# Attention values of one mixer stage: values as the stationary operand in two column groups, one product for each pair of units, and new orders of the unit loop on three engines

## The chip, the cores and the metric

One core of one Trainium2 chip runs the whole program in one launch. The metric is the device time of an execution in microseconds (us), and the number to be predicted is the median of the changed kernel's executions.

## What is computed

The reference is a network of two blocks on 256 tokens of width 1024. The first block has two layers, and each layer runs a feed-forward, a hybrid mixer, an attention over 256 memory tokens and a second feed-forward. The second block has two layers of sparse attention and a feed-forward with squared ReLU. The change lies in the hybrid mixer, which runs twice (once in each layer). What matters of it:

```
s_s = einsum('bqgrd,bqgmd->bqgrm', qi, ks) * scale - slopes * dist    # selected keys (all keys here)
o_s = einsum('bqgrm,bqgmd->bqgrd', masked_softmax(s_s), vs)
s_w = einsum('bqgrd,bkgd->bqgrk', qi, kw) * scale - slopes * dist     # window keys (all keys here)
o_w = einsum('bqgrk,bkgd->bqgrd', masked_softmax(s_w), vw)
o   = gs0 * o_c + gs1 * o_s + gs2 * o_w                              # gates; o_c: compressed keys
```

There are 8 heads of width 64 in 2 groups of 4 heads, and each group shares one set of keys and values. With 256 tokens both branches see every earlier token. The mixer's output goes through a root-mean-square norm, is joined with the output of a retention branch and multiplied by `w_out`. The keys and values of the memory attention (`xa_wk`, `xa_wv`) don't depend on the mixer, and the kernel computes them between the mixer's small steps.

## The kernel before

Large products are in three parts: each weight item of 128 x 2048 numbers is loaded by SyncE (SP) into one of four raw buffers, ScalarE (ACT) writes its rounded high part (`whi`), VectorE (DVE) writes the rest (`wlo`), and TensorE (PE) multiplies high by high, high by low and low by high. The items are taken in a fixed order. There are four raw buffers, and item i can be loaded once DVE has split item i-4. `take(s, tag, c, ahead)` splits all items up to the named one, and `memory_piece(s, p)` is one of 16 pieces of the memory keys and values: pieces 0 to 7 have 24 products of 256 columns each (two pieces use up one item of `wk`), pieces 8 to 15 have 12 products of 512 columns.

The hybrid mixer's unit loop goes over `HUNITS`, 8 units of (m, g, br): m is the block of 128 queries, br the branch (selected, window), g the group of 4 heads. Unit u has m = 0 for u < 4, with 128 keys, and m = 1 after, with 256 keys. Per unit, in order of dependence:

- PE writes scores of 4 heads to PSUM (`scores`, two units at a time at the start of units 1, 3 and 5). The heads of g = 0 lie in partitions 0 to 63 and those of g = 1 in 64 to 127, and the two units' products alternate.
- DVE adds the position terms and writes the result to SBUF (`shift`), and finds the maxima (`maximum`).
- ACT takes the exponentials (`exps`, 4 instructions with their sums).
- PE turns each head's 128 x 128 blocks (`turned`), into PSUM bank 0 for the first 128 keys and bank 1 for the others. ACT copies bank 0 to `hPT` (`h_pt` of ACT), DVE copies bank 1 (`h_pt` of DVE).
- PE multiplies: for each head and each 128 keys, the turned weights are stationary (128 x 128) and the values `vN` move (64 columns), into one half of bank 2 (`h_values`). These are float32 products; the trace shows each as two passes.
- DVE multiplies by the gate over the sum (`value`, `h_out`, 256 columns) into `tmp`, and GpSimd (POOL) adds that to `O_` (`h_sum`).

Around these steps lie two memory pieces per unit on PE (2u before the turn, 2u+1 after), their copies on ACT, and one weight item per unit on ACT and DVE (`HSPLIT`: wk 2, wk 3, wv 0 to 3, w_out 0, w_out 1). Four `blocks` calls turn the tokens for `w_out` through banks 0 and 1 (in units 2, 3 and 6, and between the products of `w_out`); ACT and DVE write their halves (`halves`). `fin` is the norm of the mixer's output. Every engine works through its own instructions in the written order and waits by semaphores, so a wait holds up everything behind it on that engine. After the loop, `eight` does the products with `w_out`.

Of the kernel before, what the change touches and what calls it, by code (L numbers as in the profile page):

```python
# [10 lines left out]
ALU = mybir.AluOpType  # L11
ACT = mybir.ActivationFunctionType
# [257 lines left out]
def build(nc, A, out):  # L270
    ctx = ExitStack()
    with ctx:
# [20 lines left out]
        R = sb("region", NREG)  # L293
# [99 lines left out]
        chid = PS[:, 6:8, 0:64].rearrange("p v (h c) -> p v h c", h=2)[:, :, :, 0:30]  # L393
        tmp = R[:, 8192:8704]
        qrT = R[:, 4096:5120].rearrange("p (k n) -> p k n", k=4)
        krT = R[:, 5120:6144].rearrange("p (k n) -> p k n", k=4)
# [152 lines left out]
        def gpsimd(e):  # L549
# [74 lines left out]
            def hybrid(s):  # L624
# [28 lines left out]
                tt(rsum.rearrange("p (m h) -> p m h", m=2), rsum.rearrange("p (m h) -> p m h", m=2), bc(r2, 4), ALU.mult, ("ret_root", l))  # L653
                for u, (m, g, br) in enumerate(HUNITS):
                    om = O_[:, m * 512 + g * 256:m * 512 + g * 256 + 256].rearrange("p (h d) -> p h d", h=4)
                    q.wait_ge(*dve.at("h_out", l, u))
                    tt(om, om, tmp[:, (u % 2) * 256:(u % 2 + 1) * 256].rearrange("p (h d) -> p h d", h=4), ALU.add, ("h_sum", l, u))
                    if u == 3:
                        q.wait_ge(*dve.at("fin_var", l, 0))
                        power(rstd[:, 0:1], var[:, 0:1], ("fin_root", l, 0))  # L660
# [48 lines left out]
        def scalar(e):  # L709
# [183 lines left out]
            def hybrid(s):  # L893
# [86 lines left out]
                take(s, "w_out", 2, 0)  # L980
# [5 lines left out]
            def fin(s, l, m):  # L986
                q.wait_ge(*pool.at("h_sum", l, 3 + 4 * m))
                q.wait_ge(*dve.at("ret_x", l, m))
                square(XN[:, m * DM:m * DM + 512], O_[:, m * 512:(m + 1) * 512], ssq[:, m:m + 1], 1.0, ("fin_sq", l, m))
# [133 lines left out]
        def vector(e):  # L1123
# [257 lines left out]
            def hybrid(s):  # L1381
# [129 lines left out]

                def value(u):
                    o = 4 * (u % 2)
                    q.wait_ge(*pe.at("h_values", l, u))
                    if u >= 2:
                        q.wait_ge(*pool.at("h_sum", l, u - 2))
# [17 lines left out]
                for u, (m, g, br) in enumerate(HUNITS):  # L1534
                    if u:
                        value(u - 1)
                    if u < 7:
                        shift(u + 1)

                    if u < 6:  # L1540
                        maximum(u + 1)
                    if m:
                        q.wait_ge(*pe.at("h_turned", l, u, 1))
                        cp(hPT[u % 2][:, 512:1024], PS[:, 1, :], ("h_pt", l, u))
                    if u == 6:
                        maximum(7)
                    if u == 0:
                        q.wait_ge(*act.at("ret_square", l))
                        red(rsum, xr[:, :, 0], ALU.add)
                        for n in range(2):  # L1550
                            h = slice(4 * n, 4 * n + 4)
                            ts(rvar[:, h], rsum[:, h], 4.0 / 128, eq[:, n:n + 1], ALU.mult, ALU.add, *([("ret_var", l)] if n else []))
                        take(s, "g_r", 1)
                    if u == 1:
                        q.wait_ge(*pool.at("ret_root", l))
                        for n in range(2):
                            tt(xr[:, n, 1], xr[:, n, 1], bc(rsum[:, 4 * n:4 * n + 4], 128), ALU.mult, ("ret_x", l, n))
                    weight(u)
                    if u == 5:
                        fin_var(s, l, 0)  # L1560
                        split_to(number[s, "wv", 3], halves=1)
                        fin(s, l, 0)
                    if u == 6:
                        halves(s + 0.5, 0, 0, 0)
                    take(s, *HSPLIT[u], 0)
                    if u == 2:
                        for h in range(2):
                            halves(s + 0.5, h, 1, h)
                value(7)
                take(s, "w_out", 2, 0)  # L1570
# [163 lines left out]
        def tensor(e):  # L1734
# [142 lines left out]

            def down(i, ah, al, first, *names):
                w = weights(i)
                for m in range(2):  # L1880
                    for kk in range(2):
                        for n in range(2):
                            down_half(w, ah, al, m, kk, n, first and kk == 0, False, *((("used", i), *names) if (m, kk, n) == (1, 1, 1) else ()))
# [15 lines left out]

            def eight(s, tag, order, waits, betweens=(), hook=None):  # L1900
                for n, c in enumerate(order[:2]):
                    q.wait_ge(*waits(c, 1))
                    down(number[s, tag, n], ahv[:, 2 * c:2 * c + 2, :], alv[:, 2 * c:2 * c + 2, :], n == 0)
# [94 lines left out]
            def memory_piece(s, p):  # L1998
                l = STAGES[s][1]
                if p < 8:  # L2000
# [3 lines left out]
                    if p >= 2:  # L2004
                        q.wait_ge(*act.at("memory", l, p - 2))
                    elif p:
                        q.wait_ge(*dve.at("g_r", l, 1))
# [13 lines left out]
            def hybrid(s):  # L2021
# [128 lines left out]
                q.wait_ge(*dve.at("m", l, 1, 1))  # L2150

                for u, (m, g, br) in enumerate(HUNITS):
                    o = u % 2
# [9 lines left out]
                    if u == 0:  # L2163
                        q.wait_ge(*dve.at("g_r", l, 0))
                    for k in range(m + 1):
                        if u == 3:
                            q.wait_ge(*dve.at("a", s + 0.5, 1, 1))
                        if k == 0 and u:
# [10 lines left out]
                    memory_piece(s, 2 * u + 1)  # L2179
                    q.wait_ge(*act.at("h_pt", l, u))  # L2180
                    if m:
                        q.wait_ge(*dve.at("h_pt", l, u))
                    if u:
                        q.wait_ge(*dve.at("h_out", l, u - 1))
# [17 lines left out]
                q.wait_ge(*act.at("memory", l, 15))  # L2202
                eight(s, "w_out", (2, 3, 0, 1), lambda c, m: dve.at("a", s + 0.5, m, c // 2), hook=second_tile)

# [234 lines left out]
```

## Time and profile before

| | us |
|---|---|
| median of 3 runs | 1832.25 (1832.12 to 1832.87) |
| the profiled execution, its own time | 1832.15 |
| its span, first to last instruction | 1830.4 |
| PE busy | 1819.6 (99% of the span) |
| DVE busy | 1306.1 (71%) |
| ACT busy | 1040.0 (57%) |
| POOL busy | 217.4 (12%) |
| granted TensorE clock | 1.000 of full speed |

The time of the profiled execution is 1.75 us longer than its span and lies 0.1 us below the median. The two unit loops lie at about 292 to 361.5 us and 914.5 to 984 us of the span. Rows of a timeline give the start, the duration, the engine, the line (a helper's: 1738 is every product, 1743 every transpose, 715 every ACT instruction), the operation, the output and inputs with their sizes, how many instructions are merged, and in brackets the idle time before them with what ended it. The duration of a product holds its way through the array; the step from one start to the next is what a product costs PE.

### The profile page before, as it was taken

What the parts mean: (1) busy time and instruction counts of PE and PEld (TensorE: products, weight loads), DVE (VectorE), ACT (ScalarE), POOL (GpSimd) and SP (SyncE); (2) the same over time, 40 slices, a digit from 0 to 9 for tenths busy, and PEclk for the clock granted to TensorE, in tenths of its full rate; (3) what the DMA queues carried; (4) which work ended last, traced back from release to release, by engine and by line L of the source; (5) the groups of instructions that cost most, each with busy time, mean ns of one, the idle gap of its engine ahead of it and who ended that gap; (6) DMA issues with size and microseconds to landing.
All of it is one profiled execution on the core that took longest, in us unless ns stands there. A gap on an engine that the chain in (4) does not pass through costs nothing.

```text
span 1830.4 us, 27037 instructions
## 1 busy us (share of the span) xinstructions
PE 1819.6 (99%) x10482; PEld 1574.9 (86%) x10482; DVE 1306.1 (71%) x1730; ACT 1040.0 (57%) x1501; POOL 217.4 (12%) x264
## 2 busy tenths in 40 slices
PE   9999999999999999999999999999999999999998
PEld 7888899888888888889998888888888888888887
DVE  6776767776766776676787677667887667787665
ACT  6555545655655565455466665555665555666543
POOL 2010102110000011001021000002100111201110
PEclk9999999999999999999999999999999999999999
DMA  9586663363755467667345356555347554645561
GB/s 321 185 295 201 169 199 118 123 216 104 237 195 189 161 211 257 228 165 238 108 156 178 127 191 213 184 178 191 144 138 230 186 197 167 217 138 174 193 197 69
DMA packets 228033, 338.03 MB, mean 185 GB/s; under 512 B 22519, under 2 KB 172161, under 8 KB 227906
## 3 DMA queue, kind: packets, MB, share of 16 engines
q1 hardware_dynamic: 220178, 307.06, 51.5%
q0 software_dynamic: 7728, 29.26, 4.8%
q8 instruction: 82, 1.34, 0.3%
q14 instruction: 45, 0.37, 0.1%
HBM read 335.25 MB, written 1.05 MB: 184 GB/s over the span
## 4 chain that ended last, share of the span: by engine, by line
PE 97%; ACT 2%; DVE 1%; issue 0%; DMA 0%; ACTq 0%; DVEq 0%
PE ps L1738 93%; PE ps L1743 3%; ACT region L715 1%; ACT whi L715 1%; ACT ahl L715 0%; DVE xn L1129 0%; DVE ahl L1129 0%; DVE wlo L1129 0%; DVE xs L1137 0%; ACT mhi L715 0%; DMA gv<-ffn_pre_g 0%; DVE nm L1133 0%; ACTq L81 0%; DVE nm L1137 0%; DVEq L81 0%
## 5 line engine op out<-in xcount | busy, mean ns | idle before, releaser
L1129 DVE TENSOR_TENSOR wlo<-raw,whi 128x1024 fp32r<-128x1024 f32 (+1 forms) x456 | 556.8, 1221 | 177.7 <-ACT whi L715 142.0
L715 ACT ACTIVATE whi<-raw 128x1024 fp32r<-128x1024 f32 (+1 forms) x456 | 479.8, 1052 | 73.2 <-PE ps L1738 33.7
L1738 PE MATMUL ps<-ahl,whi 128*128 128x512 f32 (+1 forms) x1824 | 415.8, 356 | 0.0
L1738 PEld LDWEIGHTS ps<-ahl,whi 128*128 128x128 f32 x1824 | 316.5, 190 | 42.7
L715 ACT ACTIVATE region<-ps 128x512 f32<-128x512 f32 (+2 forms) x256 | 148.7, 581 | 309.9 <-PE ps L1738 245.8
L1738 PE MATMUL ps<-whi,ahl 128*128 128x512 f32 (+2 forms) x944 | 300.2, 385 | 0.8 <-DVE ahl L1129 0.5
L1738 PE MATMUL ps<-ahl,wlo 128*128 128x256 f32 x1520 | 255.5, 282 | 0.0
L1738 PEld LDWEIGHTS ps<-ahl,wlo 128*128 128x128 f32 x1520 | 224.1, 191 | 11.9
L1738 PEld LDWEIGHTS ps<-whi,ahl 128*128 128x128 f32 x944 | 174.2, 188 | 36.6 <-DVE ahl L1129 3.4
L1129 DVE TENSOR_TENSOR mlo<-raw,mhi 128x1024 fp32r<-128x1024 f32 (+2 forms) x132 | 162.1, 1228 | 45.5 <-ACT mhi L715 36.2
L1738 PE MATMUL ps<-whi,hhi 128*128 128x512 f32 x472 | 185.6, 393 | 0.0
L1738 PE MATMUL ps<-wlo,hhi 128*128 128x512 f32 x472 | 184.3, 391 | 0.0
L1738 PE MATMUL ps<-whi,hlo 128*128 128x512 f32 x472 | 183.7, 389 | 0.0
L1738 PE MATMUL ps<-wlo,ahl 128*128 128x512 f32 (+2 forms) x472 | 178.1, 377 | 0.0
L554 POOL TENSOR_TENSOR hlo<-region,hhi 128x512 fp32r<-128x512 f32 x62 | 81.1, 1309 | 792.8 <-ACT hhi L715 792.8
L715 ACT ACTIVATE mhi<-raw 128x1024 fp32r<-128x1024 f32 (+2 forms) x132 | 138.9, 1052 | 16.2 <-PE ps L1738 7.3
L1738 PE MATMUL ps<-ahl,mhi 128*128 128x512 f32 (+1 forms) x640 | 144.4, 353 | 0.0
L1129 DVE TENSOR_TENSOR region<-region,ps 128x512 f32<-128x512 f32 x102 | 70.1, 688 | 96.1 <-ACT region L715 90.3
L715 ACT ACTIVATE hhi<-region 128x512 fp32r<-128x512 f32 x68 | 43.0, 632 | 149.4 <-DVE region L1137 76.0
L1738 PEld LDWEIGHTS ps<-ahl,mhi 128*128 128x128 f32 x640 | 111.1, 190 | 14.7
L1738 PE MATMUL ps<-region 128*128 128x64 f32 (+5 forms) x928 | 120.1, 326 | 1.1 <-ACT whi L715 1.1
L1738 PEld LDWEIGHTS ps<-region 128*128 128x128 f32 (+2 forms) x928 | 101.9, 179 | 17.2 <-issue 4.6
(172 smaller groups left out, 2356.6 us busy)
## 6 DMA issues: line engine op xcount, KB each, us to landing
raw<-w_ff SPq DMA_DIRECT2D x64, 1024.0 KB, 5.5
raw<-ffn_w_down SPq DMA_DIRECT2D x44, 1024.0 KB, 4.9
raw<-ffn_w_gate SPq DMA_DIRECT2D x40, 1024.0 KB, 5.4
raw<-ffn_w_up SPq DMA_DIRECT2D x40, 1024.0 KB, 5.7
raw<-w_in SPq DMA_DIRECT2D x34, 1024.0 KB, 6.5
raw<-w_out SPq DMA_DIRECT2D x16, 1024.0 KB, 4.9
raw<-xa_wk SPq DMA_DIRECT2D x8, 1024.0 KB, 5.1
raw<-xa_wv SPq DMA_DIRECT2D x8, 1024.0 KB, 5.0
```

What stands on the lines that cost most here:

```text
L554: e.tensor_tensor(o, a, b, op).then_inc(*pool.did(*names))
L715: e.activation(o, i, f, **kw).then_inc(*act.did(*names))
L1129: e.tensor_tensor(o, a, b, op).then_inc(*dve.did(*names))
L1738: m = e.matmul(o, l, r, start=start, stop=stop)
L1743: m = e.transpose(o, i, CS[0:k, 0:k])
```

## The change

- PE: the values of a unit are no longer computed alone. `values(j)` comes at the end of unit 2j+1 and does the units 2j and 2j+1, which have the same m and br and the groups g = 0 and 1. Now `vN` of the group is stationary (128 x 64) and `hPT` moves with 512 columns (4 heads of 128 queries). Group 0's result goes to partitions 0 to 63 of bank 2 and group 1's to 64 to 127: two column groups of the array.
- The result is turned: rows are head width, columns are queries. So ACT copies bank 2 to a new tile `OT` (`values` on ACT), PE turns it back with 4 transposes (`turn_back(j)`, in units 2, 4 and 6 just before the unit's own turn, and the last one inside the first product group of `w_out`), and DVE's `value(j)` and POOL's sum run once for two units, over 512 columns.
- ACT's order in the unit loop: the items' splits move to the head of the unit for u = 1, 2, 3, 4, 6; in units 2, 4 and 6 the exponentials of the next unit now come ahead of the unit's copy to `hPT`; `halves` of (1, 1) moves from unit 2 to unit 3.
- DVE's order: half an item's split moves ahead of `shift` in units 1 and 3, in unit 0 the split named by `take(s, "g_r", 1)` (it is item wk 1) moves ahead of the retention statistics, `maximum(7)` moves ahead of the copy in unit 6, `halves` of (1, 1) moves to unit 3.
- PE waits for ACT's `h_pt(u)` in units 2 and 6 ahead of `blocks`, since these write bank 0.

```diff
 (ACT)
+                def values(j):
+                    q.wait_ge(*pe.at("h_values", l, j))
+                    put(OT, PS[:, 2, :], ACT.Copy, ("h_values", l, j))
                 for u, (m, g, br) in enumerate(HUNITS):
+                    if u in (2, 4, 6):
+                        values(u // 2 - 1)
+                    if u in (1, 2, 3, 4, 6):
+                        take(s, *HSPLIT[u], 0)
+                    if u == 3:
+                        halves(s + 0.5, 1, 1, 1)
                     memory_piece(s, 2 * u)
+                    if u in (2, 4, 6):
+                        exps("h", l, u + 1, 128 * (HUNITS[u + 1][0] + 1), hP, 0.125)
                     q.wait_ge(*pe.at("h_turned", l, u, 0))
                     put(hPT[u % 2][:, 0:512], PS[:, 0, :], ACT.Copy, ("h_pt", l, u))
-                    if u in (1, 2, 3, 4, 5, 7):
+                    if u in (0, 1, 3, 5):
+                        exps("h", l, u + 1, 128 * (HUNITS[u + 1][0] + 1), hP, 0.125)
+                    if u == 7:
                         take(s, *HSPLIT[u], 0)
-                    if u in (5, 6):
-                        memory_piece(s, 2 * u + 1)
-                    if u < 7:
-                        exps("h", l, u + 1, 128 * (HUNITS[u + 1][0] + 1), hP, 0.125)
-                    if u not in (5, 6):
-                        memory_piece(s, 2 * u + 1)
+                    memory_piece(s, 2 * u + 1)
+                    if u in (0, 5):
+                        take(s, *HSPLIT[u], 0)
                     if u == 2:
-                        for h in range(2):
-                            halves(s + 0.5, h, 1, h)
+                        halves(s + 0.5, 0, 1, 0)
...
-                    if u in (0, 6):
-                        take(s, *HSPLIT[u], 0)
+                values(3)
 (DVE)
-                    tt(tmp[:, (u % 2) * 256:(u % 2 + 1) * 256].rearrange("p (h d) -> p h d", h=4),
-                       PS[:, 2, (u % 2) * 256:(u % 2 + 1) * 256].rearrange("p (h d) -> p h d", h=4), bc(coef[:, o:o + 4], 64), ALU.mult,
-                       ("h_out", l, u))
+                    tt(tmp.rearrange("p (g i d) -> p i g d", g=2, i=4), PS[:, 2, :].rearrange("p (i g d) -> p i g d", i=4, g=2),
+                       bc(coef.rearrange("p (g i) -> p i g", g=2), 64), ALU.mult, ("h_out", l, j))
...
-                    if u:
-                        value(u - 1)
+                    if u in (1, 3):
+                        split_to(number[s, HSPLIT[u][0], HSPLIT[u][1]], halves=1)
                     if u < 7:
                         shift(u + 1)
+                    if u == 3:
+                        halves(s + 0.5, 1, 1, 1)
-                    if u < 6:
+                    if u < 7:
                         maximum(u + 1)
+                    if u in (2, 4, 6):
+                        value(u // 2 - 1)
...
                     if u == 0:
+                        take(s, "g_r", 1)
...
 (PE)
+                def values(j):
+                    m, g, br = HUNITS[2 * j]
+                    for u in (2 * j, 2 * j + 1):
+                        q.wait_ge(*act.at("h_pt", l, u))
+                        if m:
+                            q.wait_ge(*dve.at("h_pt", l, u))
+                    if j:
+                        q.wait_ge(*dve.at("h_out", l, j - 1))
+                    for k in range(m + 1):
+                        for g in range(2):
+                            mm(PS[g * 64:(g + 1) * 64, 2, :], vN[:, k, br * 128 + g * 64:br * 128 + (g + 1) * 64],
+                               hPT[g][:, k * 512:(k + 1) * 512], k == 0, k == m, *([("h_values", l, j)] if (k, g) == (m, 1) else []))
+                def turn_back(j):
+                    q.wait_ge(*act.at("h_values", l, j))
+                    for i in range(4):
+                        turned(PS[:, 2, i * 128:(i + 1) * 128], OT[:, i * 128:(i + 1) * 128], 128, *([("h_back", l, j)] if i == 3 else []))
...
+                    if u in (2, 4, 6):
+                        turn_back(u // 2 - 1)
...
                     memory_piece(s, 2 * u + 1)
-                    q.wait_ge(*act.at("h_pt", l, u))
...
-                    for i in range(4):
-                        for k in range(m + 1):
-                            mm(PS[:, 2, o * 256 + i * 64:o * 256 + (i + 1) * 64], hPT[o][:, (k * 4 + i) * 128:(k * 4 + i + 1) * 128],
-                               vN[:, k, br * 128 + g * 64:br * 128 + (g + 1) * 64], k == 0, k == m,
-                               *([("h_values", l, u)] if (i, k) == (3, m) else []))
+                    if o:
+                        values(u // 2)
+                    if u in (2, 6):
+                        q.wait_ge(*act.at("h_pt", l, u))
```

## Rows read from the trace of the kernel before

**Rows 1.** The page: busy time of PE; the chain by engine; loads of `w_out`.

```profile
PE 1819.6 (99%) x10482; PEld 1574.9 (86%) x10482; DVE 1306.1 (71%) x1730; ACT 1040.0 (57%) x1501; POOL 217.4 (12%) x264
...
PE 97%; ACT 2%; DVE 1%; issue 0%; DMA 0%; ACTq 0%; DVEq 0%
...
raw<-w_out SPq DMA_DIRECT2D x16, 1024.0 KB, 4.9
```

**Rows 2.** Windows over both unit loops: length, busy PE, PEld, DVE, ACT, POOL.

```profile
292.00:361.50 69.50, 68.94 (x501) 62.79 (x500) 55.79 (x99) 47.70 (x100) 13.93 (x14) 1.00 0.39 131
914.50:984.00 69.50, 68.94 (x501) 62.76 (x500) 55.79 (x99) 47.70 (x100) 13.84 (x14) 1.00 0.39 131
```

**Rows 3.** Timeline of PE, first unit loop: turns, memory pieces, values.

```profile
304.38 0.60 PE L1743 MATMUL ps<-cs,region 128*128 128x128 f32 x4
304.73 0.36 PE L1738 MATMUL ps<-mhi,whi 128*128 128x256 f32 x1
...
307.69 1.00 PE L1738 MATMUL ps<-region 128*128 128x64 f32 x8
308.50 0.36 PE L1738 MATMUL ps<-mhi,whi 128*128 128x256 f32 x1
...
342.26 1.89 PE L1738 MATMUL ps<-region 128*128 128x64 f32 x16
343.96 0.48 PE L1738 MATMUL ps<-whi,mhi 128*128 128x512 f32 x1
...
346.80 1.03 PE L1743 MATMUL ps<-cs,region 128*128 128x128 f32 x8
347.59 0.47 PE L1738 MATMUL ps<-whi,mhi 128*128 128x512 f32 x1
...
359.76 1.97 PE L1738 MATMUL ps<-region 128*128 128x64 f32 x16 [0.56 <-ACT whi L715]
```

**Rows 4.** Timeline of PE: four column groups; two row groups (scores of units 4, 5).

```profile
226.75 3.66 PE L1738 MATMUL ps<-region 128*32 128x256 f32 x64
230.34 0.40 PE L1738 MATMUL ps<-whi,ahl 128*128 128x280 f32 x1
...
315.61 0.61 PE L1743 MATMUL ps<-cs,xn 128*128 128x128 f32 x4
316.15 2.00 PE L1738 MATMUL ps<-region 64*128 64x256 f32 x16
318.07 0.66 PE L1743 MATMUL ps<-cs,xn 128*128 128x128 f32 x4
```

**Rows 5.** Timeline of ACT, first unit loop: split, exponentials, copies.

```profile
305.75 2.15 ACT L715 ACTIVATE whi<-raw 128x1024 fp32r<-128x1024 f32 x2
307.99 0.40 ACT L715 ACTIVATE region<-region,sm 128x128 f32<-128x128 f32 x1
...
310.16 0.39 ACT L715 ACTIVATE region<-ps 128x256 f32<-128x256 f32 x1
...
351.33 0.51 ACT L715 ACTIVATE region<-region,sm 128x256 f32<-128x256 f32 x1
...
353.92 0.60 ACT L715 ACTIVATE ahl<-ps 128x512 fp32r<-128x512 f32 x1
```

**Rows 6.** Timeline of DVE, first unit loop: splits, value, shift and maximum.

```profile
301.87 2.56 DVE L1129 TENSOR_TENSOR wlo<-raw,whi 128x1024 fp32r<-128x1024 f32 x2
304.53 0.42 DVE L1129 TENSOR_TENSOR region<-ps,sm 128x256 f32<-128x256 f32 x1
305.06 1.25 DVE L1137 SCALAR_TENSOR_TENSOR region<-cs,ps 128x128 f32<-128x128 f32 x4
...
307.35 1.42 DVE L1129 TENSOR_TENSOR xn<-xn,sm 128x512 f32<-128x512 f32 x2
...
327.66 1.79 DVE L1137 SCALAR_TENSOR_TENSOR region<-cs,ps 128x256 f32<-128x256 f32 x4
...
331.01 0.69 DVE L1141 COPY region<-ps 128x512 f32<-128x512 f32 x1
```

More of the change, by code:

```diff
@@ L394, in build @@
         tmp = R[:, 8192:8704]
+        OT = R[:, 8704:9216]
         qrT = R[:, 4096:5120].rearrange("p (k n) -> p k n", k=4)
@@ L653, in hybrid @@
                 tt(rsum.rearrange("p (m h) -> p m h", m=2), rsum.rearrange("p (m h) -> p m h", m=2), bc(r2, 4), ALU.mult, ("ret_root", l))
[L654 to L658, printed above, removed]
+                for j in range(4):
+                    om = O_[:, (j // 2) * 512:(j // 2) * 512 + 512]
+                    q.wait_ge(*dve.at("h_out", l, j))
+                    tt(om, om, tmp, ALU.add, ("h_sum", l, j))
+                    if j == 1:
                         q.wait_ge(*dve.at("fin_var", l, 0))
@@ L986, in fin @@
             def fin(s, l, m):
-                q.wait_ge(*pool.at("h_sum", l, 3 + 4 * m))
+                q.wait_ge(*pool.at("h_sum", l, 1 + 2 * m))
                 q.wait_ge(*dve.at("ret_x", l, m))
@@ L1510, in weight, with value @@
                     tt(coef[:, o:o + 4], den[:, o:o + 4], gm[:, 4 * g:4 * g + 4, 1 + br], ALU.mult)
[L1512 to L1516, printed above, removed]
-                    tt(tmp[:, (u % 2) * 256:(u % 2 + 1) * 256].rearrange("p (h d) -> p h d", h=4),
-                       PS[:, 2, (u % 2) * 256:(u % 2 + 1) * 256].rearrange("p (h d) -> p h d", h=4), bc(coef[:, o:o + 4], 64), ALU.mult,
-                       ("h_out", l, u))
+                def value(j):
+                    q.wait_ge(*pe.at("h_back", l, j))
+                    if j:
+                        q.wait_ge(*pool.at("h_sum", l, j - 1))
+                    tt(tmp.rearrange("p (g i d) -> p i g d", g=2, i=4), PS[:, 2, :].rearrange("p (i g d) -> p i g d", i=4, g=2),
+                       bc(coef.rearrange("p (g i) -> p i g", g=2), 64), ALU.mult, ("h_out", l, j))
                 head(0)
@@ L1544, in hybrid @@
                         cp(hPT[u % 2][:, 512:1024], PS[:, 1, :], ("h_pt", l, u))
-                    if u == 6:
-                        maximum(7)
                     if u == 0:
+                        take(s, "g_r", 1)
                         q.wait_ge(*act.at("ret_square", l))
@@ L1552, in hybrid @@
                             ts(rvar[:, h], rsum[:, h], 4.0 / 128, eq[:, n:n + 1], ALU.mult, ALU.add, *([("ret_var", l)] if n else []))
-                        take(s, "g_r", 1)
                     if u == 1:
@@ L1560, in hybrid @@
                         fin_var(s, l, 0)
-                        split_to(number[s, "wv", 3], halves=1)
                         fin(s, l, 0)
+                    take(s, *HSPLIT[u], 0)
+                    if u == 2:
+                        halves(s + 0.5, 0, 1, 0)
                     if u == 6:
                         halves(s + 0.5, 0, 0, 0)
[L1565 to L1569, printed above, removed]
+                value(3)
                 take(s, "w_out", 2, 0)
@@ L1876, in down_half, with down @@
                 three(PS[:, 4 + 2 * m + n, :], ah[:, kk, ms], al[:, kk, ms], hi[:, kk, c], lo[:, kk, c], start, stop, *names)
-            def down(i, ah, al, first, *names):
+            def down(i, ah, al, first, *names, middle=None):
                 w = weights(i)
@@ L1881, in down @@
                     for kk in range(2):
+                        if (m, kk) == (0, 1) and middle:
+                            middle()
                         for n in range(2):
@@ L1898, in last_downs, with eight @@
                     down_half(w, *acts[i], m, kk, n, False, end, *names)
-            def eight(s, tag, order, waits, betweens=(), hook=None):
+            def eight(s, tag, order, waits, betweens=(), hook=None, middle=None):
                 for n, c in enumerate(order[:2]):
                     q.wait_ge(*waits(c, 1))
-                    down(number[s, tag, n], ahv[:, 2 * c:2 * c + 2, :], alv[:, 2 * c:2 * c + 2, :], n == 0)
+                    down(number[s, tag, n], ahv[:, 2 * c:2 * c + 2, :], alv[:, 2 * c:2 * c + 2, :], n == 0, middle=None if n else middle)
                     if betweens:
@@ L2005, in memory_piece @@
                         q.wait_ge(*act.at("memory", l, p - 2))
+                        if p == 7:
+                            q.wait_ge(*dve.at("a", s + 0.5, 1, 1))
                     elif p:
@@ L2202, in hybrid @@
                 q.wait_ge(*act.at("memory", l, 15))
-                eight(s, "w_out", (2, 3, 0, 1), lambda c, m: dve.at("a", s + 0.5, m, c // 2), hook=second_tile)
+                eight(s, "w_out", (2, 3, 0, 1), lambda c, m: dve.at("a", s + 0.5, m, c // 2), hook=second_tile, middle=lambda: turn_back(3))
             def memory(s):
```

7 lines of the change are left out of this document (2 added, 5 removed).

## The prediction

> **What bounds the kernel now.** I read the page first: PE is busy for 99% of the span, and the chain of waits that ends last is 97% PE [rows 1]. So a change counts by two things: what it takes from PE's own work, and what waits it gives PE. Next I took the windows over the two unit loops. They are alike to 0.1 us: 69.5 us long, PE busy 68.9, DVE 55.8, ACT 47.7 [rows 2]. So each number below is worked out in the first loop and counted twice. The other engines have slack as a mean (14 us on DVE, 22 us on ACT), but they work in a written order, and whether PE waits is settled by the order. The timeline of PE shows one wait in the loop of before: 0.56 us ahead of unit 7's values [rows 3]. Everything else follows without a gap, so there is hardly any idle time to win, and each new wait costs its full length. The sum is made against the profiled execution's 1832.15 us, 0.1 below the median of the runs.
>
> **PE's own work, per loop.** Taken away: the values of a unit take 0.81 us with 128 keys (307.69 to 308.50) and 1.70 us with 256 keys (342.26 to 343.96) [rows 3]. Four of each: 10.0 us. The wait of 0.56 goes too: in the new order unit 7's DVE copy is no longer behind a late split, I find it done over 1 us before PE asks.
>
> Added, products: no row has two column groups with 512 columns. The nearest is the compression's product in four column groups with 256 columns: 64 passes from 226.75 to 230.34, 3.59 us [rows 4]. One after the other, at the 0.22 us that I find below, they would need 14 us; so four groups run side by side, in 16 rounds of 0.22 us. The scores in two row groups give the same: 16 passes in 1.92 us are 8 rounds and a rest [rows 4]. A round of 512 columns is twice that, 0.44 us. The new values have 2 passes for each 128 keys, both groups together: 2+2+4+4 = 12 rounds, 5.2 us. If the groups did not overlap it would be 24 rounds, 10.5 us; that is the upper bound. I take 5.2, the row being of the same kind.
>
> Added, going into and out of a split array: before the scores the 4 transposes step 0.54 us (315.61 to 316.15) where 4 transposes elsewhere step 0.35 (304.38 to 304.73), and 1.92 is 0.16 more than 8 rounds [rows 3, 4]. That is 0.35 us each time; four blocks of values make 1.3 us (bounds 0.5 and 2). The Trainium skill (TensorEngine Tiling (Array Packing), Key Properties) says that changing the tiling mode drains TensorE, without a figure; the 0.35 us agrees with it. The same page (When to Use Tiling) names this very swap for narrow moving operands, with up to 2 times the speed: by that alone the values would go from 10.0 to 5.0 us and the sum would be some 1.5 us per loop better than mine before waits.
>
> Added, turning back: 4 transposes 0.35 us alone, and 0.44 more where they stand ahead of others (8 take 0.79, 346.80 to 347.59) [rows 3]. Three times 0.44 and once 0.35: 1.7 us.
>
> PE's work: -10.0 + 5.2 + 1.3 + 1.7 = -1.8 us per loop.
>
> **New waits.** I walk the three queues by the steps of the rows: ACT's four exponentials 2.17 us with 128 keys (307.99 to 310.16) and 2.59 with 256 (351.33 to 353.92), an item's split 2.24 (305.75 to 307.99), a copy of 256 columns 0.39 and of 512 columns 0.60, each plus 0.09 to the next [rows 5]; DVE's split 2.66 or 1.33 for half (301.87 to 304.53), shift and maximum together 2.29 (305.06 to 307.35) and 3.35 (327.66 to 331.01) [rows 6]. PE's pieces are 2.96 (304.73 to 307.69) and 2.84 us (343.96 to 346.80) [rows 3]. From a release to PE's product I allow 0.15 us.
>
> *Unit 2.* PE gets to unit 1's turn 0.81 us earlier, at 303.57 instead of 304.38. Then 0.35 + 2.96, values(0) 0.87 + 0.32, piece 4 2.96: 311.0, where turn_back(0) wants `OT`. On DVE, the work up to 301.87 is the same in another order. Then come item wk 2 (to 304.53), the moved half of wk 3 (305.86), shift and maximum of unit 2 (308.15). So ACT's exps(2) start at 308.2, as late as before (307.99), though PE is earlier. exps(2) 2.17, copy 0.48, `OT` 0.60: ready at 311.45, PE goes on at 311.6. **Wait 0.6 us.** Behind it stand 8 transposes and piece 5: 311.6 + 0.79 + 2.96 = 315.35. There PE waits for h_pt(2), since blocks(0,1,0) writes bank 0. ACT now puts much in front of that copy: after `OT` (311.54) the split of wv 0 2.24, a copy 0.48, exps(3) 2.17, and only then h_pt(2) 0.60: 317.03. PE goes on at 317.2. **Wait 1.8 us.** Behind it on PE are the blocks, the scores of units 4 and 5 and all pieces. In before the same blocks start at 315.61 [rows 4]; they come 1.6 us later.
>
> *Unit 3.* Piece 7 newly waits for DVE's half (1,1), which now stands behind half (0,1), half an item and shift(4): ready about when PE comes. **Wait 0.2 us.** Units 4 and 5: turn_back(1)'s `OT` copy follows exps(4) and is done 2 us before PE asks; no wait.
>
> *Unit 6.* I count from the end of the scores of units 6 and 7, S. PE turns unit 5 after piece 10; h_pt(5) is done at S+4.1; exps(6) 2.59, copy 0.69: S+7.4. The split of wv 3 now follows here instead of preceding exps(6). DVE can split after ACT's first half: S+8.5, 2.66 more: S+11.2; shift(7) and maximum(7) stand behind that: S+14.5. exps(7): S+17.1, and then h_pt(6): S+17.7, PE at S+17.9. PE itself needs 2.84 + 0.79 + 2.84, values(2) 1.74 + 0.32, piece 12 2.84, turn_back and turn 1.23, piece 13 2.84: S+15.4. **Wait 2.4 us** before blocks(0,0,0). Piece 14 then waits for ACT's copy of piece 13, one copy behind h_pt(6): **0.3 us** more. In before h_pt(6) came right behind the turn, so exps(7) could be this late and PE never saw it.
>
> *The tail.* Turn_back(3) stands 1.4 us inside w_out's first group, and `OT` is ready by then. value(3), POOL's sum, fin and its root follow; I find `fin` done 4 us before PE's last blocks. POOL has half as many sums, twice as wide, beside an engine that has to wait for nothing: no cost. Loads take 4.9 us [rows 1]; that of w_out 3 comes later by the delay of wv 3's split (3 us), with 15 us to spare: no cost.
>
> Waits: 0.6 + 1.8 + 0.2 + 2.7 = 5.3 us, less the 0.56 that goes: +4.7. Net per loop: +4.7 - 1.8 = +2.9 us. Twice: +5.8, so 1832.15 + 5.8 = **1838 us**, 0.3% slower. Each wait is a difference of sums over 10 to 17 us; a step's error of 2% moves it by 0.3 us, and the two loops err together: 1835.9 to 1840.5 for this case.
>
> **Rivals.**
> - *The column groups do not overlap.* 5.2 us more product time per loop. Of it, what lies ahead of the waits of units 2 and 6 (0.87 + 1.74) is swallowed by them, and the other 2.6 adds: 1838 + 5.2 = 1843 us. Against it stand the 64 passes in 3.59 us [rows 4]. Chance 0.06.
> - *One wait comes out small*, most likely that of unit 6, if DVE reaches shift(7) 2.7 us earlier than I find. 1838 - 5.4 = 1832.6 us, no change. For it: my walk holds no contention or luck between engines. Against: its steps follow without idle time on ACT or DVE in long stretches. Chance 0.18.
> - *The other side: the copies to `hPT` are in time everywhere.* What decides is one thing: ACT has to finish h_pt(2) by 315.2 and h_pt(6) by S+15.3, which takes exps(3) and exps(7) done about 2 us earlier. For it speaks ACT's mean slack of 22 us in 69.5 [rows 2]. Then only PE's work counts: 1832.15 - 2 x (1.8 + 0.56) = 1827.4 us. Chance 0.14.
>
> **How the numbers follow.** Chances: the forecast 0.62, the others 0.06, 0.18 and 0.14. A measurement here can tell 0.2%, 3.7 us. Slower by over 0.2% (above 1835.9): the forecast and the first rival less a little at the edge, 0.64. Within 0.2%: the second rival and that edge, 0.20. Faster (under 1828.6): the third rival and a little of the second, 0.16. The range reaches down over the second rival and up over most of what a 2% error and a worse overlap can add: 1830 to 1842 us. It leaves out the third rival and the first.
>
> **What would show it.** In the new trace, per loop: 24 passes of 512 columns with a 128 x 64 stationary, in steps of 0.44 us for two; PE idle about 0.6 us before the turn of unit 2, 1.8 us before blocks of unit 2 and 2.4 us before those of unit 6, each ended by an ACT copy; no wait before the last values; PE's busy time down by some 3 to 4 us in all and its idle time up by 9 to 10 us. I am wrong if ACT's copies h_pt(2) and h_pt(6) start right behind their turns, or if the passes of the two groups follow one another.

## The result, and the profile after

The changed kernel takes **1841.2 us** (median of 6 runs, 1838.39 to 1842.79); before takes 1832.7 on the same chip (6 runs, 1832.12 to 1833.46). The ratio is 1.0046 (95%: 1.0036 to 1.0055): slower by almost half a per cent. The profiled execution of after took 1842.79 us with a span of 1841.0, against 1832.15 and 1830.4 before: 10.6 us more span.

The page of after: busy times, and the chain by engine.

```profile
PE 1821.5 (99%) x10370; PEld 1563.5 (85%) x10370; DVE 1309.5 (71%) x1722; ACT 1044.9 (57%) x1509; POOL 215.2 (12%) x256
...
PE 94%; DVE 4%; ACT 1%; issue 0%; DMA 0%; DVEq 0%; ACTq 0%
```

The chain was 97% PE [rows 1] and is 94%; DVE's share of it went from 1 to 4%. The view of waits says where, for PE over the whole span and then over the first unit loop (total us, times, longest):

```profile
PE ps L1752 <- ACT region L716: 10.4, 6, 2.1
```

```profile
PE ps L1752 <- ACT region L716: 5.1, 3, 2.1
```

Six waits, three per loop, each ended by an ACT copy. The timeline of PE in the first loop shows them, and the new values:

```profile
307.04 1.08 PE L1747 MATMUL ps<-region 128*64 128x512 f32 x4
308.05 0.38 PE L1747 MATMUL ps<-mhi,whi 128*128 128x256 f32 x1
...
312.54 1.06 PE L1752 MATMUL ps<-cs,region 128*128 128x128 f32 x8 [1.36 <-ACT region L716]
...
318.05 0.66 PE L1752 MATMUL ps<-cs,xn 128*128 128x128 f32 x4 [1.57 <-ACT region L716]
...
344.14 1.94 PE L1747 MATMUL ps<-region 128*64 128x512 f32 x8
346.01 0.50 PE L1747 MATMUL ps<-whi,mhi 128*128 128x512 f32 x1
...
348.91 1.47 PE L1752 MATMUL ps<-cs,region 128*128 128x128 f32 x12
350.14 0.47 PE L1747 MATMUL ps<-whi,mhi 128*128 128x512 f32 x1
...
355.26 0.66 PE L1752 MATMUL ps<-cs,xn 128*128 128x128 f32 x4 [2.12 <-ACT region L716]
355.95 0.80 PE L1747 MATMUL ps<-whi,mhi 128*128 128x512 f32 x1
356.54 0.63 PE L1747 MATMUL ps<-wlo,mhi 128*128 128x512 f32 x1
...
359.10 0.50 PE L1747 MATMUL ps<-wlo,mhi 128*128 128x512 f32 x1
359.44 0.39 PE L1747 MATMUL ps<-whi,mlo 128*128 128x512 f32 x1
...
364.07 1.94 PE L1747 MATMUL ps<-region 128*64 128x512 f32 x8
```

Two things are to be read here. First, the waits: 312.54 is turn_back(0), 318.05 the first block of unit 2, 355.26 that of unit 6. Every wait of PE in the text from here on is taken from the start of the last product ahead to the next start, less the same step where nothing waits. So these take 1.52, 1.73 and 2.29 us (in the second loop 1.52, 2.02 and 2.28). The last values, at 364.07, wait for nothing; in before they lost 0.56 by the view [rows 3], 0.72 from start to start. The view of waits leaves out delays that the rest of a product's way through the array covers. The starts show two such in the first loop: piece 7, behind the turn of unit 3 (323.93), starts at 324.49, 0.20 late and 0.06 after DVE's half (1,1) is done (323.74 and 0.69 us); piece 14 starts at 355.95, some 0.25 late and 0.05 after ACT's copy of piece 13 (the second of the two from 354.61). The second loop has neither. Second, the step of the products **behind** the wait of unit 6: 0.43 us from 356.54 on, where the same products before and after it step 0.23. The windows say what that is (the columns of [rows 2]; the eighth is the granted clock):

```profile
292.00:366.00 74.00, 68.90 (x442) 56.01 (x441) 57.97 (x95) 48.47 (x102) 12.14 (x10) 0.98 0.38 129
...
355.30:359.30 4.00, 3.97 (x12) 3.06 (x13) 2.09 (x3) 1.19 (x2) 0.00 (x0) 0.57 0.27 72
359.30:363.30 4.00, 4.00 (x23) 3.37 (x22) 1.55 (x4) 2.18 (x3) 0.00 (x0) 1.00 0.50 193
945.00:949.50 4.50, 4.13 (x21) 2.88 (x22) 3.50 (x5) 3.41 (x5) 0.00 (x0) 0.66 0.41 113
984.00:988.00 4.00, 4.00 (x13) 3.38 (x14) 2.13 (x3) 1.20 (x2) 0.00 (x0) 0.58 0.26 69
```

In before the granted clock is 1.00 over both loops [rows 2]. In after it falls to its lower level (1.2 GHz instead of 2.4) in three places, each right behind one of the waits: 12 PE instructions in 4 us, then 23 in the next 4. The place at 945 shows it on another operation: the scores of units 4 and 5 took 1.92 us in before [rows 4] and 3.3 here, with no wait inside:

```profile
945.96 3.39 PE L1747 MATMUL ps<-region 64*128 64x256 f32 x16
949.28 0.90 PE L1752 MATMUL ps<-cs,xn 128*128 128x128 f32 x4
```

What the three places cost, from these windows: 0.43 x 4.0 + 0.34 x 4.5 + 0.42 x 4.0 = 4.9 us. The rest of the 10.6 is then 5.7, and the forecast's sum was 5.8; that they agree so well is partly luck, as the section on the prediction shows term by term. That is why PE's **busy** time did not fall by 3 to 4 us as forecast but rose by 1.9: products at the lower clock count as busy. Its idle time rose by 8.7 us (19.5 against 10.8), where 9 to 10 were forecast. The runs fit this: the fastest (1838.39) had a mean granted clock of 0.999, the two slowest (1842.79, 1842.63) 0.996.

### The profile page after: what moved, and what is told of

Same layout as the page of the kernel before. It is cut to its first block, busy times and chain, and to the rows that moved or that the text cites. A ratio compares the mean times of both kernels' runs of the same rounds, so it can differ in the third digit from the quotient of the medians.

```text
span 1841.0 us, 26795 instructions
## 1 busy us (share of the span) xinstructions
PE 1821.5 (99%) x10370; PEld 1563.5 (85%) x10370; DVE 1309.5 (71%) x1722; ACT 1044.9 (57%) x1509; POOL 215.2 (12%) x256
## 4 chain that ended last, share of the span: by engine, by line
PE 94%; DVE 4%; ACT 1%; issue 0%; DMA 0%; DVEq 0%; ACTq 0%
PE ps L1747 91%; PE ps L1752 3%; DVE wlo L1140 1%; ACT region L716 1%; DVE region L1148 1%; DVE sm L1156 0%; DVE xn L1140 0%; DVE sm L1144 0%; DVE xs L1148 0%; DVE ahl L1140 0%; ACT whi L716 0%; DMA gv<-ffn_pre_g 0%; ACT ahl L716 0%; DVE sm L1160 0%; DVE region L1140 0%
## 5 line engine op out<-in xcount | busy, mean ns | idle before, releaser
L716 ACT ACTIVATE region<-ps 128x512 f32<-128x512 f32 (+3 forms) x264 | 153.5, 582 | 306.4 <-PE ps L1747 238.2
L1747 PE MATMUL ps<-region 128*128 128x256 f32 (+6 forms) x784 | 110.6, 361 | 0.0
L1747 PEld LDWEIGHTS ps<-whi,hlo 128*128 128x128 f32 x472 | 88.6, 188 | 19.0
```

Source lines behind the costliest of these rows:

```text
L716: e.activation(o, i, f, **kw).then_inc(*act.did(*names))
L1747: m = e.matmul(o, l, r, start=start, stop=stop)
```

## What made the first wait 1.5 us

PE came to turn_back(0) at 311.0, as forecast. Late were ACT's exps(2), at 309.15 instead of 308.2, behind DVE's shift(2). Timeline of DVE, and the row of POOL beside it:

```profile
297.15 3.46 DVE L1140 TENSOR_TENSOR wlo<-raw,whi 128x1024 fp32r<-128x1024 f32 x2
300.65 1.22 DVE L1156 TENSOR_REDUCE sm<-xn 128x8 f32<-128x1024 f32 x1
...
302.91 3.93 DVE L1140 TENSOR_TENSOR wlo<-raw,whi 128x1024 fp32r<-128x1024 f32 x3
306.94 1.25 DVE L1148 SCALAR_TENSOR_TENSOR region<-cs,ps 128x128 f32<-128x128 f32 x4
```

```profile
297.17 2.36 POOL L555 TENSOR_TENSOR xn<-xn,region 128x512 f32<-128x512 f32 x1
```

A split is two instructions of 1.23 us; here it took 3.46. POOL's multiplication, 1.29 us elsewhere in the same trace, took 2.36 beside it. In before DVE had the sum over `xn` at this time, and POOL's row read 1.30:

```profile
297.09 1.22 DVE L1145 TENSOR_REDUCE sm<-xn 128x8 f32<-128x1024 f32 x1
```

```profile
297.11 1.30 POOL L554 TENSOR_TENSOR xn<-xn,region 128x512 f32<-128x512 f32 x1
```

The change moved the split of `wk` 1 ahead of that sum, into POOL's way; both lost 1.0 us, in the manner of two that take turns: half a split (1.23), the multiplication (1.3, held up 1.07), the other half. The Trainium skill (SBUF — State Buffer, SBUF: two separate sides) states it: VectorE with two operands in SBUF and GpSimd share one pair of ports, held for a whole instruction. These two rows agree; in before the sum over `xn`, with one operand, ran beside POOL at its usual 1.22. Experiment 5, which among other things puts this split back behind the sum, has 2.48 and 1.30 us again; experiment 10, which leaves it where the change put it, has 3.46 and 2.36.

ACT's and DVE's rows around the later two waits:

```profile
312.49 2.15 ACT L716 ACTIVATE whi<-raw 128x1024 fp32r<-128x1024 f32 x2
...
315.23 0.40 ACT L716 ACTIVATE region<-region,sm 128x128 f32<-128x128 f32 x1
...
317.40 1.07 ACT L716 ACTIVATE region<-ps 128x512 f32<-128x512 f32 x2
...
345.05 2.15 ACT L716 ACTIVATE whi<-raw 128x1024 fp32r<-128x1024 f32 x2
...
352.01 0.51 ACT L716 ACTIVATE region<-region,sm 128x256 f32<-128x256 f32 x1 [1.87 <-DVE sm L1144]
...
354.61 1.29 ACT L716 ACTIVATE region<-ps 128x512 f32<-128x512 f32 x2
```

```profile
346.14 2.56 DVE L1140 TENSOR_TENSOR wlo<-raw,whi 128x1024 fp32r<-128x1024 f32 x2 [1.78 <-ACT whi L716]
348.73 1.78 DVE L1148 SCALAR_TENSOR_TENSOR region<-cs,ps 128x256 f32<-128x256 f32 x4
```

They read as the forecast's walk: in unit 2 h_pt(2) (317.40) stands behind the split and exps(3). In unit 6 the split of wv 3 (345.05) holds DVE's half until 346.14, shift(7) until 348.73, exps(7) until 352.01 and h_pt(6) until 354.61, though ACT was idle for 1.87 us ahead of exps(7).

## The experiments

All but the sixth are edits of the changed kernel, the sixth is one of before; all compute the whole result. Cuts of the code are marked by "...". Each was timed in 3 to 5 rounds beside before on the same chip, whose median there was 1832.72, 1832.78 or 1832.27. The theory: the time is lost in three waits made by the order on ACT and DVE, and in the clock behind them. The rivals: the new products themselves are dear, or the waits are of another origin.

**1. The split of wv 3 back ahead of exps(6).** On ACT:

```diff
-                    if u in (1, 2, 3, 4, 6):
+                    if u in (1, 2, 3, 4, 5, 6):
                         take(s, *HSPLIT[u], 0)
...
-                    if u in (0, 5):
+                    if u == 0:
                         take(s, *HSPLIT[u], 0)
```

> The changed kernel with one edit: in unit 5 ACT splits item wv 3 ahead of the exponentials of unit 6, as before the change. Order theory (the loss is made of waits that the new orders of ACT and DVE give PE): by the walk of the queues the wait in front of unit 6's blocks falls from 2.3 to about 0.8 us per loop, the others stay; 3.2 us less in all, and one of the two long waits of each loop is gone, so fewer stretches at half the granted clock behind it: 1841.2 falls to 1835.5, between 1834 and 1838. Product theory (the loss is the new products' own cost): no change, 1841. Clock theory as part of the order theory: no stretch at half clock behind unit 6 in the profile.

Measured 1836.48 (1836.27 to 1838.72), ratio 1.0023 (1.0014 to 1.0032). The wait of 2.3 before unit 6's blocks is gone, one of 0.86 before piece 12 has come in its place; the waits of unit 2 stay at 1.52 and 1.73 (1.52 and 2.01 in the second loop). Only one place at the lower clock is left, behind unit 2 in the second loop. So one misplaced split was worth 4.7 us.

**2. Units 2 and 3 alone.** On ACT h_pt(2), piece 5 and the moved half of the next block's item come ahead of exps(3); on DVE the halves of wk 3 and wv 1 go back behind shift and maximum.

```diff
 (ACT)
-                    if u in (2, 4, 6):
+                    if u in (4, 6):
                         exps("h", l, u + 1, 128 * (HUNITS[u + 1][0] + 1), hP, 0.125)
...
                         halves(s + 0.5, 0, 1, 0)
+                        exps("h", l, 3, 128, hP, 0.125)
 (DVE)
-                    if u in (1, 3):
-                        split_to(number[s, HSPLIT[u][0], HSPLIT[u][1]], halves=1)
-                    if u < 7:
-                        shift(u + 1)
                     if u == 3:
                         halves(s + 0.5, 1, 1, 1)
+                    if u < 7:
+                        shift(u + 1)
```

(In ACT's unit 3 that half also moves ahead of the item's split.)

> The changed kernel with new orders in units 1 to 3 alone: ACT copies unit 2 to hPT and does its blocks' half before the exponentials of unit 3, takes half (1,1) first in unit 3; DVE takes half (1,1) first in unit 3 and has no early half split in units 1 and 3. Order theory: the waits of 1.4 and 1.6 us in unit 2 go, 2.8 us per loop less by the walk, 5.6 in all, and the long wait in front of unit 6's blocks stays with its half-clock stretches: about 1835, between 1833 and 1837. Product theory: 1841.

Measured 1836.79 (1835.13 to 1837.19), ratio 1.0020 (1.0011 to 1.0029). Both waits of unit 2 are gone; that of unit 6 is left with 2.33 us, and 0.44 at 335.24. The clock falls behind unit 6 in both loops, and nowhere else in them.

**3. Both, and `fin_var` and `fin` of unit 5 ahead of its copy on DVE.**

> Both edits together, and in unit 5 the norm of the output before DVE's copy. The products are those of the changed kernel. Order theory: PE waits only 0.6 us per loop, 5.1 us per loop less than the changed kernel before the clock is counted; PE's own work is 1.8 us per loop under that of the kernel before: 1828 us, 4 to 5 us faster than the kernel before, full granted clock all through. Product theory: not under 1835. Serial column groups: about 1838.

Measured 1831.40 (1831.02 to 1832.31), ratio 0.9993 (0.9984 to 1.0002): level with before, about 10 us under the changed kernel with the same products on PE. So the products are not what made it slow. But it missed its expectation by 3.4 us. ACT's timeline shows why:

```profile
334.61 0.63 ACT L716 ACTIVATE xn<-region 128x512 f32<-128x512 f32 x1
337.71 2.15 ACT L716 ACTIVATE whi<-raw 128x1024 fp32r<-128x1024 f32 x2 [2.38 <-PE ps L1747]
```

The split of wv 3 waits 2.38 us for **PE**: its home comes free only when piece 10 has read what is in it. My walk had when the split is wanted, and not when its home is free. Everything on ACT then stands 2.4 us later, and the copy of piece 11 lets PE wait 0.83 us before piece 12 (0.44 more after the scores of units 6 and 7, 0.50 at piece 14). The expectation of experiment 7 has the first and the last as 1.1 and 0.4, because it takes off the step between two products of a kind instead of the step at that place.

**4. Products in place of the waits.** The orders of the change stay. PE gets products that nobody reads (they write a bank that is free there) just ahead of the three waits. By their steps they take 1.2, 1.4 and 1.8 us, somewhat less than the waits.

```diff
+                def fill(n):
+                    for _ in range(n):
+                        mm(PS[:, 4, :], MHI[:, 0:128], MHI[:, 0:512], True, True)
...
+                    if u == 2:
+                        fill(5)
                     if u in (2, 4, 6):
                         turn_back(u // 2 - 1)
...
                     if u in (2, 6):
+                        fill(6 if u == 2 else 8)
                         q.wait_ge(*act.at("h_pt", l, u))
```

> The changed kernel with products that nothing reads (5, 6 and 8 of 512 columns into a free PSUM bank, 4.3 us per loop) put where PE would wait in units 2 and 6. They do not shorten any wait, they fill it. Clock theory: the granted clock stays full, the runs scatter less, and the time is that of the waits alone, 1837.5 us (1836.5 to 1839). Without a clock effect: 1841, or more if the filler delays PE.

```profile
311.18 1.43 PE L1747 MATMUL ps<-mhi 128*128 128x512 f32 x5
...
316.19 1.55 PE L1747 MATMUL ps<-mhi 128*128 128x512 f32 x6
317.95 0.66 PE L1752 MATMUL ps<-cs,xn 128*128 128x128 f32 x4 [0.21 <-ACT region L716]
```

Measured 1838.87 (1838.57 to 1839.67), against the changed kernel's 1841.2 (1838.39 to 1842.79), which ran on another chip. The first block of unit 2 starts at 317.95, 0.1 us earlier than without the products: ACT, not PE, sets that time. The granted clock is 1.00 in both loops, the profiled span 1836.8, which is 4.2 less than that of after. **More work on PE, less time.** What the waits cost by their mere length stays; the drop of the clock behind them is gone, and with it most of the scatter (1.1 us instead of 4.4). The ranges of the two overlap: the fastest run of the changed kernel (1838.39), with a mean clock of 0.999, is level with this one. The gain is one against its other runs, in which the clock was lower.

**5. The new products with the old orders.** ACT and DVE as in before, with the copy to `OT` at the head of units 2, 4 and 6 and the value behind the maximum.

> The new products (pairs, column groups, turn back) with the orders of ACT and DVE of the kernel before; only the copy of the sums goes to the head of units 2, 4 and 6 on ACT, and the gate product stands behind the maximum on DVE. Order theory: PE's own work is 1.8 us per loop lower, new waits of some 3.3 us per loop (copies of pieces 9 and 13, half (0,0) before unit 7's turn), the wait of 0.7 us before the last values goes: 0.7 us per loop over the kernel before, 1834 us (1832.5 to 1836). Product theory: the whole loss of 8.5 us is here too, 1841.

Measured 1835.33 (1835.10 to 1837.65), ratio 1.0015 (1.0006 to 1.0024). The waits are others (the first loop has 0.82 before `wk` 1's piece, 0.41 in unit 2, 1.16 at 337.12, 0.50 and 1.25 in unit 7), none reaches 1.3 us, and the clock stays at 1.00. So with the old orders the new products cost 2.5 us more than before, and the change with its own orders 5.9 more on top: the new orders are the larger part of the loss. The 2.5 are waits too, as experiments 9 and 10 show with the same products.

**6. The order alone, on the kernel before.** Its exps(3) and exps(7) go ahead of h_pt(2) and h_pt(6), nothing else.

```diff
                     memory_piece(s, 2 * u)
+                    if u in (2, 6):
+                        exps("h", l, u + 1, 128 * (HUNITS[u + 1][0] + 1), hP, 0.125)
                     q.wait_ge(*pe.at("h_turned", l, u, 0))
...
-                    if u < 7:
+                    if u < 7 and u not in (2, 6):
                         exps("h", l, u + 1, 128 * (HUNITS[u + 1][0] + 1), hP, 0.125)
```

> The kernel before, with its own products, and one edit of the new order: in units 2 and 6 ACT does the exponentials of the next unit ahead of the copy to hPT. Order theory: PE waits 2.9 and 3.1 us per loop for that copy, the wait at unit 7 goes: 5.1 us per loop, 10.3 in all, and 1 to 2 us more for each of up to four stretches at half clock: 1843 to 1850 us. Product theory: no more than noise beside 1832.7.

```profile
PE ps L1740 <- ACT region L715: 10.4, 4, 2.7
```

```profile
318.61 1.10 PE L1740 MATMUL ps<-region 128*128 128x64 f32 x8 [2.50 <-ACT region L715]
```

Measured 1848.87 (1848.16 to 1851.21), ratio 1.0090 (1.0076 to 1.0104). Four waits, 2.64 to 2.88 us each from start to start, make 11.0 of the 18.8 us that the profiled span has more; the granted clock is 0.96 over the first loop (290 to 372 us) and 0.94 over the second (912 to 996 us), which is 3.3 and 5.0 us. The three together are a little over the 18.8, since the wait of before in each loop is gone. It makes before slower by nearly twice what the whole change does: the place of exps(u+1) against h_pt(u) is enough by itself.

**7. The orders written again.** Experiment 3, and in unit 5 ACT has copy, split of wv 3, copy of piece 11, exps(6), so that the split stands where its home is free; the split of `w_out` 0 goes to the end of unit 6.

```diff
-                    if u in (1, 2, 3, 4, 5, 6):
+                    if u in (1, 2, 3, 4):
                         take(s, *HSPLIT[u], 0)
...
-                    if u in (0, 1, 3, 5):
+                    if u in (0, 1, 3):
                         exps("h", l, u + 1, 128 * (HUNITS[u + 1][0] + 1), hP, 0.125)
-                    if u == 7:
+                    if u in (5, 7):
                         take(s, *HSPLIT[u], 0)
                     memory_piece(s, 2 * u + 1)
+                    if u == 5:
+                        exps("h", l, 6, 256, hP, 0.125)
...
                         halves(s + 0.5, 0, 0, 0)
+                        take(s, *HSPLIT[u], 0)
```

> As e3, with ACT's order in units 5 and 6 changed again: wv 3 is split behind the copy to hPT (its home is freed only by piece 10), the copy of piece 11 comes ahead of the exponentials of unit 6, w_out 0 is split at the end of unit 6. The walk, now with the wait for the split's home in it, gives e3 1.0 us of wait at piece 12 and 0.6 at piece 14, which its trace shows as 1.1 and 0.4. Here it gives 0.5 before unit 6's blocks and 0.3 at piece 14: 0.8 us per loop less than e3, 1829.8 us (1828.5 to 1831). Product theory: nothing under 1832.

Measured 1838.09 (1836.89 to 1838.97), ratio 1.0029 (1.0017 to 1.0040): a miss of 8 us. PE, then DVE:

```profile
357.53 1.50 PE L1755 MATMUL ps<-cs,region 128*128 128x128 f32 x8 [2.15 <-DVE ahl L1144]
```

```profile
354.20 2.56 DVE L1144 TENSOR_TENSOR wlo<-raw,whi 128x1024 fp32r<-128x1024 f32 x2 [3.60 <-ACT whi L716]
356.79 0.69 DVE L1144 TENSOR_TENSOR ahl<-ps,ahl 128x512 fp32r<-128x512 f32 x1
```

DVE waits 3.60 us for the split that I had moved back on ACT, and behind it stands a half (0.69 us) that PE wants next. I had moved the split on one engine and left it in its place on the other. The clock falls behind this wait in both loops.

**8. The same with h_pt(6) ahead of exps(7) on ACT.**

> As e7, and in unit 6 too the copy to hPT comes ahead of the exponentials of unit 7. By the walk the wait moves from the blocks to piece 14, which waits for the copy of piece 13 (0.75 us): same as e7 within 0.3 us, 1829.8. If only the copy to hPT mattered it would be 1 us faster than e7.

Measured 1835.47 (1834.89 to 1837.95), ratio 1.0016 (1.0007 to 1.0025). The wait behind DVE's half is the same, 2.29 us, so this misses its expectation by 5.7 us for the same reason. But the clock falls behind it in the first loop only. In the second the wait is as long, and the clock stays (the last line is a window, the eighth number the clock):

```profile
981.54 1.09 PE L1755 MATMUL ps<-cs,region 128*128 128x128 f32 x8 [2.14 <-DVE ahl L1144]
...
985.00:989.00 4.00, 4.00 (x19) 1.97 (x18) 1.47 (x2) 2.28 (x4) 0.00 (x0) 1.00 0.29 67
```

**9 and 10. The half ahead of the split on DVE too,** in 7 and in 8:

```diff
+                    if u == 6:
+                        halves(s + 0.5, 0, 0, 0)
                     take(s, *HSPLIT[u], 0)
...
-                    if u == 6:
-                        halves(s + 0.5, 0, 0, 0)
```

> As e7, and in unit 6 DVE does the half (0,0) ahead of the split of w_out 0, as in the kernel before (the changed kernel has it behind, and e7 moved that split later, which made the wait of 2.3 us before unit 7's turn). Order theory: that wait goes, 0.5 us before unit 6's blocks and 0.3 at piece 14 remain, no stretch at half clock in the loops: 2.5 us per loop under the kernel before by the walk, less 0.4 that e7 shows at piece 10: 1828.6 us (1827.5 to 1830). Product theory: nothing under 1832.

> The same edit on e8. By the walk as e9, with one wait of 0.75 us at piece 14 in place of two: 1828.6 us (1827.5 to 1830).

Measured 1829.82 (1829.52 to 1832.59), ratio 0.9989 (0.9980 to 0.9997), and **1829.46** (1829.14 to 1830.23), ratio 0.9984 (0.9975 to 0.9993). One swap of two DVE operations gave 8.3 and 6.0 us, 0.5 of which is the other chip (before took 1832.78 there and 1832.27 here). The page, the waits in the first loop, and DVE's timeline of experiment 10:

```profile
PE 1816.5 (99%) x10370; PEld 1559.7 (85%) x10370; DVE 1309.4 (72%) x1722; ACT 1044.8 (57%) x1509; POOL 214.8 (12%) x256
```

```profile
PE ps L1750 <- ACT region L716: 0.7, 2, 0.4
```

```profile
351.72 0.69 DVE L1144 TENSOR_TENSOR ahl<-ps,ahl 128x512 fp32r<-128x512 f32 x1 [2.30 <-ACT ahl L716]
352.88 2.55 DVE L1144 TENSOR_TENSOR wlo<-raw,whi 128x1024 fp32r<-128x1024 f32 x2 [0.46 <-ACT whi L716]
```

The half is done at 352.4 instead of 357.5. This is the best version: 2.8 us (0.16%) under before on its chip and some 11.5 under the changed kernel.

## Why the prediction came out as it did

The direction, and the mechanism, are shown: PE waits for the copies h_pt(2), h_pt(6) and for turn_back(0), because of the written orders. Experiments 1, 2 and 6 take the waits away or make them alone. The time came 3.2 us above the number. It lies in the range, near its upper end, but above the 1835.9 to 1840.5 that the forecast gave for its own case: the room at the top was meant for errors of the walk and a worse overlap, and the lower clock used it up. That the range held is partly luck. Step by step:

- **Rounds.** Forecast 0.44 us, both column groups side by side. Read: 1.87 - 1.01 = 0.86 us for two rounds more, 0.43 each. The passes of the two groups start 0.01 us apart. Right; the rival of groups in turn falls, also by experiments 3, 9 and 10, which have the same products and are not slower than before.
- **Going into and out of the split array.** Forecast 0.35 for each block of values. 1.01 is two rounds and 0.15, and a start comes 0.09 late (343.82 to 344.14 where the step is 0.23): 0.24. The term was a little too large.
- **Turn-backs.** Forecast 0.44 where they stand ahead of others: 12 transposes took 1.23 (348.91 to 350.14), 8 took 0.79 [rows 3]: 0.44. Right.
- **PE's work, the sum.** Forecast -1.8 us per loop (12 x 0.44 and 4 x 0.35 are 5.3 and 1.4, and not the 5.2 and 1.3 that it added, so -1.6 by its own terms). By these parts it is 2 x 1.10 + 2 x 1.96 + 1.7 - 10.0 = -2.2. By the whole it comes out the same, in experiment 10, at full clock: from the scores of units 0 and 1 to the second blocks of `w_out` its first loop takes 79.13 us and its second 79.45, where before takes 80.57 and 80.60. Waits, from start to start, are 1.40 and 1.75 of the first two (0.18 at turn_back(0), 0.19 at turn_back(1), 0.44 before piece 10, 0.59 before piece 14, and in the second loop also 0.37 in unit 3) and 0.72 of each of the others. That leaves -2.1 and -2.2. So the term was 0.3 to 0.4 us per loop too small.
- **First wait of unit 2.** Forecast 0.6, measured 1.52. This is the step that was mis-sized. "The work up to 301.87 is the same in another order" priced a reordering of DVE at nothing; the split beside POOL took 1.0 us longer. That it is these two engines' conflict is read from the trace; no run moved the split alone (experiment 5 moved it with others).
- **Second wait of unit 2, and that of unit 6.** Forecast 1.8 and 2.4; measured 1.73 and 2.29 (2.02 and 2.28 in the second loop). Right. The second did not grow with the late first one, since ACT and PE were late together.
- **Unit 3 and piece 14.** Forecast 0.2 and 0.3. In the first loop 0.20 and some 0.25, ended by the two operations that the forecast named; in the second nothing. In experiment 1, at full clock there, piece 14 waits 0.50.
- **The wait of before that goes.** Forecast 0.56, by the view; 0.72 from start to start; gone.
- **The sum of these.** Waits: forecast 5.3 us per loop, measured 6.0 and 5.8. Less the wait that goes, and with PE's work, the two loops come to about 3.1 and 2.9 us without the clock, where 2.9 was forecast (the rest of the span is some 0.4 shorter, which gives the 5.7). The first wait was 0.9 too short, PE's own gain 0.3 to 0.4 too small, and the errors largely cancel.
- **What the sum had no term for:** the clock. "Each new wait costs its full length" was too little. In the profiled execution, behind three of the six long waits, the products ran at 1.2 GHz, which took 4.9 us. Experiment 4 shows it apart: with the waits filled by products, 2.3 us less in the median and 4.2 in the profiled span; its 1838.87 is 0.9 above the forecast. [Rows 2] had the clock at 1.00, and I took it as given, though the forecast itself put waits into the loops. The Trainium skill (TensorE: Matmul & The Clock Gate, Part 1: The HAM clock gate) ties the clock to how busy TensorE has recently been; by it the forecast should have had a rival in which the clock falls behind new waits. The trace agrees with the direction.

The rival "copies in time everywhere" (1827.4) is what experiments 9 and 10 nearly build (1829.8 and 1829.5): the exchange of the products is a gain of two to three us, where the orders around it let it be. What is open is what decides on the clock in a single execution. In the unit loops of these traces the waits of 2.01 to 2.88 us had it fall behind them in 13 cases of 14, and those of up to 1.73 us in none. The one exception, 2.3 us in the second loop of experiment 8, says that the length alone does not settle it.

## What to carry to other kernels

In a kernel whose bounding engine is 99% busy, write down for each of its steps what it waits for and where that stands in the other engines' queues; here a copy of 0.6 us that stood behind four exponentials cost PE 1.7 to 2.9 us each time. Move an operation on every engine that has a share in it, ask when its home is free, and ask who else uses the engine's memory at the new time. Price a new wait at its length, and then at up to 1.7 us more for the lower clock behind it; waits of up to 1.73 us had no such cost in these runs, and one of 2.3 us had none either.

## What was not expected of the hardware

- PE at 99% busy over the span still had its clock halved behind single waits of 2.0 to 2.9 us; with 19 products more per loop that nobody reads the median fell from 1841.2 to 1838.9 us.
- A DVE split (twice 1.23 us) and a POOL multiplication (1.29) that met took 3.46 and 2.36, though neither reads what the other writes.
- Two column groups with 512 moving columns run side by side (both passes start within 0.01 us, 0.43 us per round; no run has one group alone to compare); 24 passes of them took the place of 96 narrow ones in each loop.
